# Expert stage: the next job's tiles turned one chunk sooner, the sums of its inputs in sixteen pieces among the accumulations

## The reference, cut to what matters

```
h = jax.nn.silu(lax.ragged_dot(xs, w1, sizes)) * lax.ragged_dot(xs, w3, sizes)
y = lax.ragged_dot(h, w2, sizes) * gates.reshape(-1)[order][:, None]
```

## Time and profile before

| | us |
|---|---|
| three timed runs | 9104.96, 9092.64, 9102.00 |
| their median | 9102.0 |
| the profiled execution | 9096.15 |
| its span, first to last instruction | 9094.3 |

### The profile page before, as it was taken

How to read it: one execution, slowest core, us unless ns; L and a number is a source line. 1 busy time by engine, 2 the same in 40 slices (tenths; PEclk the granted TensorE clock), 3 DMA queues, 4 the chain that set the end, 5 groups by cost and what they waited for, 6 DMA issues and landing times. The chain is left out here.

```text
span 9094.3 us, 121111 instructions
## 1 busy us (share of the span) xinstructions
PE 8529.6 (94%) x43014; PEld 6135.5 (67%) x43014; DVE 3846.0 (42%) x8193; ACT 1563.8 (17%) x3792; POOL 2796.7 (31%) x2389
## 2 busy tenths in 40 slices
PE   8975899999999999897999999999999999999994
PEld 4444566647767776544777777777777777777773
DVE  2336455433343434544444444444444344343334
ACT  1124222221010101122222222211010000000002
POOL 0011000003343433112544445444444333333333
PEclk9986999999999999997999999999999999999997
DMA  5312100035555543224444444444444333333325
GB/s 231 135 48 75 33 5 6 23 127 197 194 204 199 201 164 100 79 90 145 157 166 164 164 166 157 166 153 153 143 152 140 116 131 111 132 130 116 112 97 205
DMA packets 700514, 1201.64 MB, mean 132 GB/s; under 512 B 30322, under 2 KB 533026, under 8 KB 693367
## 3 DMA queue, kind: packets, MB, share of 16 engines
q1 hardware_dynamic: 644700, 987.05, 32.3%
q0 software_dynamic: 55584, 211.54, 6.0%
HBM read 959.01 MB, written 237.39 MB: 132 GB/s over the span
## 5 line engine op out<-in xcount | busy, mean ns | idle before, releaser
L2803 PE MATMUL ex_ps<-ex_w,ex_a 128*128 128x512 f32 (+2 forms) x5376 | 1684.8, 540 | 60.8 <-DVE ex_ya L2993 60.8
L2803 PEld LDWEIGHTS ex_ps<-ex_w,ex_a 128*128 128x128 f32 (+2 forms) x5376 | 686.6, 163 | 949.9 <-issue 847.5
L2701 POOL TENSOR_TENSOR ex_sm<-ex_w 128x512 f32<-128x512 f32 x392 | 496.8, 1267 | 2623.4 <-PE ex_ps L2758 2590.3
L2758 PE MATMUL ex_ps<-ex_tx,ex_w 128*128 x6272 | 952.3, 295 | 26.2 <-DVE ex_tmp L2949 26.1
L2758 PE MATMUL ex_ps<-ex_xt,ex_w 128*128 x6272 | 962.3, 297 | 14.3 <-issue 12.0
L2758 PEld LDWEIGHTS ex_ps<-ex_xt,ex_w 128*128 128x128 f32 x6272 | 872.6, 192 | 112.7 <-issue 112.7
L2993 DVE TENSOR_TENSOR ex_ya<-ex_ps,ex_ya 128x512 f32 x910 | 602.5, 665 | 728.6 <-PE ex_ps L2803 728.6
L2758 PEld LDWEIGHTS ex_ps<-ex_tx,ex_w 128*128 128x128 f32 x6272 | 863.2, 191 | 39.5 <-issue 20.7
L2758 PE MATMUL ex_ps<-ex_tx,ex_sm 128*128 x6272 | 886.4, 295 | 2.6 <-DVE ex_tx L2912 2.6
L2758 PEld LDWEIGHTS ex_ps<-ex_tx,ex_sm 128*128 128x128 f32 x6272 | 846.4, 192 | 2.9 <-issue 2.9
L694 PE MATMUL de_ps<-de_w,de_big 128*128 128x512 f32 x1408 | 619.3, 597 | 24.5 <-DVE de_big L911 24.5
(11 more groups left out here) (403 smaller groups left out, 10613.5 us busy)
## 6 DMA issues: line engine op xcount, KB each, us to landing
ex_w<-in_o_w SPq DMA_DIRECT2D x594, 1024.0 KB, 5.0
de_wr<-in_e_w SPq DMA_DIRECT2D x88, 1024.0 KB
xs<-de_zero POOLq DMA_DIRECT2D x136, 512.0 KB, 4.6
ys<-de_zero POOLq DMA_DIRECT2D x136, 512.0 KB, 5.4
en_ch<-in_w_mod SPq DMA_DIRECT2D x48, 1024.0 KB, 5.2
de_w<-in_e_w SPq DMA_DIRECT2D x44, 1024.0 KB
ex_x<-xs SPq DMA_DIRECT2D x60, 512.0 KB, 5.0
proj<-en_o POOLq DMA_DIRECT2D x18, 1008.0 KB, 4.1
```

The costliest lines, as they stand in the source:

```text
L2701: nc.gpsimd.tensor_tensor(SM[:, w, 0], A11, A21, ALU.subtract).then_inc(sums["s3"], 1)
L2758: last = nc.tensor.matmul(PS[:, bank, 0:h], left[:, k], right[k], start=start and k == 0, stop=k == HK - 1, skip_group_check=not start)
L2803: last = nc.tensor.matmul(PS[c * rows_n:(c + 1) * rows_n, 4 + o % 3, 0:width], A[:, b, r0:r0 + rows_n], W2[:, s, b, c0 + c * width:c0 + (c ...
```

## The change: what it does

The turning moves from chunks FC - 2 and FC - 1 to FC - 3 and FC - 2, on TensorE, VectorE and ScalarE. The four sums become sixteen pieces of 224 elements. Eight pieces (out 0 and out 2) are put between the additions of chunk FC - 2, eight (out 1 and out 3) between those of chunk FC - 1: after addition number o of `per`, the pieces from 8*o//per up to 8*(o+1)//per. The last piece raises `t_made`. For the first job all sixteen run in a row. More chunks are written out: four on TensorE (FC - 4 to FC - 1; the loop has one pass fewer), three on ScalarE and on VectorE. "Four job sizes" in the name of the change is what the kernel before has too.

```diff
+    TURNS = {FC - 3: tuple(range(TILES)), FC - 2: tuple(range(TILES, 2 * TILES))}
...
-                    with pe.Fori(0, FC // 2 - 1) as q:
+                    with pe.Fori(0, FC // 2 - 2) as q:
...
-                    for s in range(2):
-                        chunk(FC - 2 + s, s, ..., hooks=tuple(range(4 * s, 4 * s + 4)))
+                    for f in range(FC - 4, FC):
+                        chunk(f, f % 2, ..., hooks=TURNS.get(f, ()))
...
-                    with act.Fori(0, FC - 2) as f:
+                    with act.Fori(0, FC - 3) as f:
                         chunk(f)
-                    for s in range(2):
-                        chunk(FC - 2 + s, tuple(range(4 * s, 4 * s + 4)))
+                    for f in range(FC - 3, FC):
+                        chunk(f, TURNS.get(f, ()))
...
+            def sum_parts(j, at, step):
...
+                if step == 0:
+                    dve.wait_ge(half_a, tiles)
+                    dve.sem_inc(passed_dve, 1)
+                    dve.wait_ge(half_v, tiles)
+                    dve.sem_inc(passed_dve, 1)
...
+                def made(part):
+                    k = part % HK
+                    if step == 0 and part < HK:
+                        last = nc.vector.tensor_tensor(out(0, k), quarter(0, 1, k), quarter(0, 0, k), ALU.subtract)
+                        if k == HK - 1:
+                            last.then_inc(a_part, 1)
+                    elif step == 0:
+                        nc.vector.tensor_tensor(out(2, k), quarter(1, 1, k), quarter(0, 1, k), ALU.subtract)
+                    elif part < HK:
+                        if k == 0:
+                            dve.wait_ge(a_part, j * 2 + 1)
+                        last = nc.vector.tensor_tensor(out(1, k), quarter(1, 1, k), out(0, k), ALU.subtract)
+                        if k == HK - 1:
+                            last.then_inc(a_part, 1)
+                    else:
+                        if k == 0:
+                            dve.wait_ge(a_part, j * 2 + 2)
+                        last = nc.vector.tensor_tensor(out(3, k), out(1, k), quarter(1, 0, k), ALU.subtract)
+                        if k == HK - 1:
+                            last.then_inc(t_made, 1)
...
-                        if hooks and hooks[-1] == 2 * TILES - 1:
-                            token_sums(dve.snap((j + 1).with_bounds(min_val=1, max_val=JOBS)), other)
+                        following = None
+                        if late in (FC - 2, FC - 1):
+                            following = dve.snap((j + 1).with_bounds(min_val=1, max_val=JOBS))
+                            parts_made = sum_parts(following, other, late - (FC - 2))
...
                                 nc.vector.tensor_tensor(out, new, out, ALU.add).then_inc(y_added[t], 1)
+                            if following is not None:
+                                for part in range(8 * o // per, 8 * (o + 1) // per):
+                                    parts_made(part)
...
-                    with dve.Fori(1, FC - 2) as f:
+                    with dve.Fori(1, FC - 3) as f:
                         chunk(f)
-                    for s in range(2):
-                        chunk(FC - 2 + s, hooks=tuple(range(4 * s, 4 * s + 4)))
+                    for f in range(FC - 3, FC):
+                        chunk(f, hooks=TURNS.get(f, ()), late=f)
```

More of the change, by code:

```diff
@@ L2806, in chunk @@
                             last.then_inc(y_done[t], 1)
-                    with pe.Fori(0, FC // 2 - 1) as q:
+                    with pe.Fori(0, FC // 2 - 2) as q:
                         for s in range(2):
                             chunk(q * 2 + s, s, pe.snap((j * (FC // 2) + q).with_bounds(min_val=0, max_val=JOBS * FC)))
-                    for s in range(2):
-                        chunk(FC - 2 + s, s, pe.snap((j * (FC // 2) + (FC // 2 - 1)).with_bounds(min_val=0, max_val=JOBS * FC)),
-                              hooks=tuple(range(4 * s, 4 * s + 4)))
+                    for f in range(FC - 4, FC):
+                        chunk(f, f % 2, pe.snap((j * (FC // 2) + f // 2).with_bounds(min_val=0, max_val=JOBS * FC)), hooks=TURNS.get(f, ()))
         @block.scalar
@@ L2887, in take @@
                 last.then_inc(half_v, 1)
-            def token_sums(j, at):
-                half = listed(dve, 2, j, HM) if not isinstance(j, int) else dve.value_load(CT[0:1, 2, j:j + 1], min_val=0, max_val=HM)
+            def sum_parts(j, at, step):
+                early = isinstance(j, int)
+                half = dve.value_load(CT[0:1, 2, 0:1], min_val=0, max_val=HM) if early else listed(dve, 2, j, HM)
                 pick = at if isinstance(at, slice) else bass.ds(at, 1)
[L2893 to L2900, removed]
-                    cols_b = bass.ds(half, HM) if b else slice(0, HM)
[L2902 to L2912, removed]
@@ new lines, in sum_parts, with quarter, out @@
+                tiles = TILES if early else j * TILES + TILES
+                if step == 0:
[3 more added lines that the diff above has]
+                    dve.sem_inc(passed_dve, 1)
+                def quarter(a, b, k):
+                    cols_b = bass.ds(half, HM) if b else slice(0, HM)
+                    return XT[:, pick, a * HK + k, cols_b].rearrange("p a n -> p (a n)")
+                def out(q, k):
+                    return TX[:, pick, q, k].rearrange("p a n -> p (a n)")
@@ L2914, in _ @@
+                return made
             for x in range(0, 2 * TILES, 2):
                 take(x, 0, slice(0, 1))
-            token_sums(0, slice(0, 1))
+            for step in range(2):
+                made = sum_parts(0, slice(0, 1), step)
+                for part in range(2 * HK):
+                    made(part)
             nc.vector.reciprocal(GK[:, 0], GG[:, 2]).then_inc(share, 1)
@@ L2976, in combine, with chunk @@
                             hidden("c12", 0, 1, 1, slot(1), a_second)
-                    def chunk(f, first=False, hooks=()):
+                    def chunk(f, first=False, hooks=(), late=None):
                         g = dve.snap((j * FC + f).with_bounds(min_val=0, max_val=JOBS * FC))
```

## The result

| | us |
|---|---|
| changed kernel, median of 4 runs | 9039.6 (9038.5 to 9047.7) |
| the kernel before, same chip, 4 runs | 9102.6 (9092.6 to 9105.0) |
| ratio | 0.9940, 95% interval 0.9928 to 0.9952 |
| profiled execution, span | 9047.7, 9045.9 |

The change gains 0.6%, 63 us, where 90 were forecast: the sign is right, but the time is outside the forecast's own range of 8998 to 9020. It lies inside the wider range of 8998 to 9042, which was given for the forecast and its rivals together.

The account below looks back on a forecast made before the run. PE, busy 94% of the span, bounds the kernel; only its idle time and clock can give time back. Terms sum to 90.4 us gained, 9102.0 to about 9012; own range 8998 to 9020 (58%), wider range 8998 to 9042.

Parts of the forecast that it names:

- five changes within 128: Job changes at h = 128: 27.2 us each would become 21.1, 30.6 us gained over five.
- two of 144: Job changes at h = 144: 58.7 us together would become 44.8, 13.9 us gained, with p6 waiting 0.55.
- three of 176: Job changes at h = 176: 101.9 us together would become 3 x 26.8, 21.5 us gained, p6 waiting 0 to 0.1.
- three size changes: Where job size changes, p1 starts sooner after the last chunk's outputs: 35.8 us together against 54.6, 18.8 gained.
- table loads and loop pass: One ScalarE chunk with table loads fewer per h = 128 job, 3.7 us; one TensorE loop pass fewer per job, 1.4.
- what the wait and its clock cost: At h = 128 changes, 4.57 us waiting before output part four plus 2.7 of clock; afterwards p6 waits 1.45, no clock loss.
- the turns with GpSimd: Two-SBUF-operand instructions of VectorE and GpSimd alternate, so the first three of a chunk's eight pieces wait for GpSimd.
- The slower rival: Each VectorE piece, not only a chunk's first three, loses a 1.27 us turn to GpSimd: 9270 us, chance 4%.
- one pass of TensorE's loop fewer: TensorE's job loop: about 0.1 us gained in each of 14 jobs, 1.4 us in all, bounds 0 and 2.
- a longer body: TensorE's six-chunk body makes five loop-backs at h = 144 and 176 wait for fetches, 12 us: 9024, chance 20%.
- own sign of being wrong: PE idle by issue ahead of p1, packets in size repeats; clock 0.5 within a size; L2949 of chunk 13 over 0.7 late.
- The rival's other figure: TensorE's loop-backs: if all ten changes within a size pay a 3.3 us fetch wait, 9045 us.

Follow-up runs that it names:

- e7: Changed kernel with TensorE's body back at four chunks, half the turning between output parts, and all 14 ScalarE chunks written out: 8966.0 us.
- e1: Kernel before with one TensorE loop pass written out, six chunks in the job body instead of four, turning and sums unmoved: 9139.2 us.
- e5: Changed kernel with each chunk's eight pieces ahead of its first addition instead of among the additions: 9152.3 us.
- e6: Changed kernel with half the turning between output parts and all pieces in chunk 13, TensorE's body kept at six chunks: 9047.0 us.
- e8: Changed kernel with 128 unused semaphore increments on TensorE ahead of the stage, moving later instructions by 128 places: 9047.0 us.
- e2: Changed kernel with one more TensorE loop pass written out, eight chunks in the job body instead of six: 9028.1 us.

## Why the prediction was right or wrong, point by point

| term | forecast | measured |
|---|---|---|
| five changes within 128 | 30.6 | 29.1 |
| two of 144 | 13.9 | 3.8 |
| three of 176 | 21.5 | -3.2 |
| three size changes | 18.8 | 18.0 |
| table loads and loop pass | 5.1 | 4.5 (the rest) |
| together, on the stage | 89.9 | 52.2 |

The size changes are measured from the last chunk's outputs to the next job's first, clock included; on the forecast's own stretch, to the next p1, they gain 19.9 (54.6 before, 34.8 now). The fifth line is what the others leave of the 52.2. In each of the six jobs of 128 the chunks ahead of the last are together 0.61 us shorter, which is the forecast 3.7; at the other sizes, where the prediction took the table loads to be hidden, none run (e7). For the loop pass e1, where it stands alone, shows some 0.6 in all jobs, not 1.4.

**Right: what the wait and its clock cost.** The thirteen waits of 4.57 and the last job's 1.5 went, and an undisturbed change of 128 takes 20.4, better than the forecast 21.1. p6 waits 0.8 and not 1.45: the overlap of pieces with GpSimd's instructions was a little kinder than my steps. The clock stayed at 1.00 through p6's waits of 0.8, as the earlier trace rows had it, and at the changes of 128 also through the issue waits of 1.0 to 3.0.

**Right: the turns with GpSimd.** Three pieces of eight are lengthened, as the steps had it, none of the others. The slower rival's price would need all eight. e5 shows what was at stake: with the same pieces ahead of the additions the kernel is slower than before.

**Wrong: the loop passes.** The step that failed is the sentence that counts 1.4 us gained for "one pass of TensorE's loop fewer". It took the pass's branch and put the body's length at nothing in the sum, leaving it to a rival with 20%. That rival, "a longer body", was the case: 37.7 us missing, against 36.8 and 43.7 for the longer body alone (e6, e1). The prediction's own sign of being wrong is what the profile shows: PE idle by "issue" ahead of p1, packets in repeats of a size, the clock at 0.5 within a size. Counted from the trace, TensorE's body had 1224, 1360 and 1432 instructions at 128, 144 and 176, and from the second job of a size to its last no q8 packet was fetched. The prediction had estimated some 1300 before and some 1920 after, at h = 176. The body now has 1765, 1969 and 2077, and 27 packets are fetched during the five further jobs of 128.

**The rival was itself sized too low**, 12 us for 38. Its 2.5 us per change was one wait, at five changes. At 144 a change pays 3.9 (issue) and then has the clock at half for 3.4 us, 5.1 lost in all; at 176 there are two waits, 3.7 and 1.9 to 2.5, with the clock at half for 6.8: 8.2 lost. And three changes of 128 pay 1.0 to 3.0 where I had them free. The rival's other figure, 9045 for ten changes at 3.3 each, comes near the measured 9039.6 by luck: eight changes paid, at 1.0 to 8.2.

The Trainium skill (Runtime: NRT & Kernel Launch, Instruction fetch mechanics) gives TensorE 2048 instructions in blocks of 256. The runs agree with its direction, packets of 16384 bytes and a wait where the job loop goes back. They show refetching already at 1765 instructions, under its figure, and none at 1432. The same section says that a taken branch to a place outside a window of two pages forces a fetch. For TensorE that is not borne out: bodies of 1224 to 1432 instructions, five to six such blocks, went round without a packet.

**Left open.** Where between 1432 and 1765 the limit lies; why a change of 128 pays mostly 1.0 to 1.4 and one of 144 mostly 3.4 to 4.0; what TensorE waits for after the packet has ended; and why the second wait follows four matmuls into p1 (e8 shows only that moving the body removes it). No run was made for these.

## What to carry to other kernels

When a change writes out more of a loop, count the instructions of the whole outer body on that engine, and look whether fetch packets appear in its repeats: here 540 to 650 more instructions took back two fifths of the forecast gain on the stage. Small work for a shared engine belongs between the instructions that free the bottleneck's buffers, not ahead of them. A wait on TensorE is priced with the clock that it can cost behind it, 4.57 and 2.7 us here.

## What the runs showed of the hardware that was not expected

A body over the limit costs none, one or two waits per return, not one in proportion to its length: eight chunks in the body were 14 us faster on the stage than six. Placing the same code 128 instructions later took the second wait from the changes of 176 and gave one to each change of 128. Which changes of 128 are free differs between two profiles of the same kernel.

The clock behind such a wait isn't the same each time. At the change from 128 to 144 TensorE waits 3.47 us in the changed kernel and in e2; in the first it then runs at half clock for 6.8 us, in the second not at all, and the stretch is 27.4 against 24.3.

At h = 128 ScalarE loads a table twice in each pass of its loop, 1.28 us each. That costs TensorE 0.6 us per chunk, 39 us in all, though ScalarE is busy for 17% of the time. The loops of the other sizes, from the same source lines, have no table load; no run shows why.
